# A transformer block pair on one core: x by features, projections ahead of its norm

## The chip, the core and the metric

The kernel runs on one core of a Trainium2 chip. The metric is device time in microseconds (us). The engines are called PE (TensorE), DVE (VectorE), ACT (ScalarE), POOL (GpSimd) and SP (SyncE, which here only issues transfers).

## The reference

Two transformer blocks are applied to x, 512 tokens of 1024 features, all fp32. What the change touches is the first stage of the first block, and a filter that the second block needs:

```python
h = rms_norm(x, g_mix_pre)                 # x * rsqrt(mean(x*x) + eps) * gain, per token
proj = h @ w_in                            # 1024 x 5376
q, k, v, p_in, gm_u, gm_v, gate_in = split(proj)
o_sb = stick_breaking_attention(q, k, v)
o_pool = multiscale_pool(p_in, ...)        # trailing sums over tokens
o_gm = gelu(gm_u) * (W_s @ norm(gelu(gm_v)) + b)
...
h = sin(freq * (z @ w1 + b1)); h = sin(freq * (h @ w2 + b2)); h = sin(freq * (h @ w3 + b3))
h = (h @ w4) * exp(-t * deltas)            # 512 taps x 2048: filters of the second block
```

The norm's factor is one number per token, the gain one per feature. So `(x * gain) @ w * factor` equals `rms_norm(x) @ w`.

## The kernel before

**Products in two halves.** Each fp32 operand of a large product is split into a rounded high part and a low part (fp32r); a product is three matmuls of 512 columns, high by high, high by low, low by high (`mm3`, line 460). Weights come as units of 128x1024 (0.5 MB): SP loads a unit into one of four `RAW` buffers (line 2552), ACT copies it rounded to `WH` (line 1108, semaphore `w_hi`), DVE subtracts to `WL` (line 1687, `lo`). There are four slots of each, so unit u waits until PE has begun unit u-3 (`w_used`). Each engine's own program says by a call `weights(u)` where among its other work it handles unit u, and it works strictly in that order.

**The start.** SP issues four transfers for x by tokens (0.5 MB each), the constants, `pp` (per-feature numbers), four weight units, and the filter's inputs. ACT squares and sums x (line 1122); DVE scales x by its norm's factor (line 1702); PE turns it with 32 transposes (`turn_x`, line 521, 16 of them within the first projection); ACT and DVE read the turned tiles from PSUM, times the gain, into `HTh` and `HTl` (lines 1130, 1708), eight tiles of 128 features by 512 tokens.

**The first stage** is a loop over k = 0..19 in each of the four programs; each k has a `first(k)` and a `second(k)`. On PE:

- k = 0 to 3: one block of `w_in` for p_in (k 0, 1) or gm_u (k 2, 3), 24 matmuls (`feature_group`, line 534, units 0 to 3). ACT brings the result out of PSUM, with gelu for gm_u (lines 1139, 1141).
- k = 4: first gm_v (`token_step`, 96 matmuls of 256 columns, units 4 and 5), then block 0 of q and k. k = 4 to 11 are the eight blocks j = k - 4 of q and k, one unit each (6 to 13). ACT copies a block out (line 1151), DVE subtracts (line 1721).
- k = 12 to 19: v (units 14 to 17), and at 16 to 19 a `mix` product of the pooled and the gated branch.

`second(k)` on PE is one layer of the filter network at k = 0, 1, 2 (`filter_layer`, line 568: a small fp32 matmul, then seven DVE instructions, lines 1733 to 1742, then a Sin on ACT, line 1163), and one of eight tap steps at k = 3 to 10 (`taps`, line 579). A tap step t is a pair of fp32 matmuls into banks 6 and 7. DVE multiplies both by the decay (line 1753, `tap_mul`), into two buffers; POOL writes their sum and difference (line 2359, `tap_ed`); SP stores them (line 2597). Step t may use the banks on PE once DVE has read step t-1, and DVE may write the buffers once POOL is done with step t-1. Steps 2i and 2i+1 use one decay, an Exp of 128x2048 on ACT into a single buffer (line 1170), taken after DVE's last use of the one before. After the last tap step POOL computes the trailing sums (line 2369), which the mix at k = 16 needs.

The attention's scores begin at k = 18, and all that follows is in the order that PE's program gives.

Of the kernel before, what the change touches and what calls it, by code (L numbers as in the profile page):

```python
# [7 lines left out]
F32R = mybir.dt.float32r  # L8
# [156 lines left out]
class Waits:  # L165
# [5 lines left out]
    def wait_ge(self, name, n):  # L171
        s, before = self.find(name)
        if n > 0 and self.past.get(s.name, 0) < before + n:
# [14 lines left out]
          "lp": tuple((n, 2) for n in ("nc", "n3", "n4")),  # L188
# [5 lines left out]
CHAINS = {"p_turn": (("p_n1", 8), ("p_n2", 8), ("p_nc", 4), ("p_n3", 8), ("p_n5", 4), ("p_n4", 8)),  # L194
# [8 lines left out]
          "p_subn": (("p_sub", 1), ("p_sn", 4)),  # L203
# [4 lines left out]
          "v_gate": (("eg_raw", 6), ("eg_mul", 4), ("ef_v", 8), ("g_mul", 18)),  # L208
# [15 lines left out]
          "g_wide": (("o2_xp", 6), ("dn_xp", 14)),  # L224
          "p_qk2": (("p_q2", 4), ("p_kx", 4)),
# [45 lines left out]
def program(nc, a):  # L271
    ctx = ExitStack()
    with ctx:
# [21 lines left out]
        SPL = [at("spl", k, [P, 1280], F32R) for k in (10, 168)]  # L295
        WT = [at("wt", 3 * i, [P, 6, P]) for i in range(2)]
# [9 lines left out]
        DELT, DEC = at("delt", 128, [P, CHUNK]), at("dec", 144, [P, CHUNK])  # L306
# [129 lines left out]
        def tensor_program(engine):  # L436
# [82 lines left out]
            e.wait_ge("d_c", 32)  # L519

            def turn_x(k):
                b = bank(("n1", k), "n1_lo", k + 1, tuple(range(8)))
                for i in range(4):
                    e.wait_ge("n1_xn", i + 1)
                    m = tp(PS[:, b, i * P:(i + 1) * P], Y[:, i, k * P:(k + 1) * P])
                m.then_inc(sem("p_n1"), 1)

            for k in range(4):
                turn_x(k)


            RING6, RING2 = tuple(range(6)), (6, 7)

            def feature_group(key, s, n, c, ready, done):
                b = bank(key, s, n, RING6)
                for k in KT:
                    if key == ("proj", 0) and k < 4:
                        turn_x(k + 4)
                    e.wait_ge(ready, k + 1)
                    m = mm3(PS[:, b, :], weights("w_in", k * P, c), HT(k), k == 0, k == 7)  # L540
                m.then_inc(sem(done), 1)

            def token_step(key, k, c, w, done):
                wk = weights("w_in", k * P, c)
                for i in range(4):
                    h, l = HT(k)
                    m = mm3(PS[:, BANK[key, i], :w], (h[:, i * P:(i + 1) * P], l[:, i * P:(i + 1) * P]), wk, k == 0, k == 7)
                    if k == 7:
                        m.then_inc(sem(done), 1)

            def first(k):
                if k < 4:
                    feature_group(("proj", k), "proj_ev", k + 1, 1536 + k * P, "n1_lo", "p_proj")
                elif k < 12:
                    if k == 4:
                        for i in range(4):
                            bank(("gmv", i), "gmv_ev", i + 1, RING6)
                        for kk in KT:
                            token_step("gmv", kk, 2048, 256, "p_gmv")
                    j = k - 4  # L560
                    feature_group(("qk", j), "qk_lo", j + 1, j * P, "n1_lo", "p_qk")
                else:
# [3 lines left out]
                    token_step("v", k - 12, 1024, S, "p_v")  # L566
# [12 lines left out]
            def taps(i, o):  # L579

                n = 4 * i + 2 * o
# [512 lines left out]
        def scalar_program(engine):  # L1094
# [29 lines left out]
            e.wait_ge("d_c", 32)
            weights(0)
            for k in KT:
                if k % 4 == 0:
                    weights(k // 4)
                e.wait_ge("p_n1", k + 1)
                act(HTh[:, k, :], PS[:, BANK["n1", k], :], ACT.Copy, scale=pp("g_mix_pre", k)).then_inc(sem("n1_hi"), 1)  # L1130
            act(SILU, pp("c_2", 0, 16), ACT.Silu).then_inc(sem("silu"), 1)
# [1666 lines left out]
```

## Time and profile before

| | us |
|---|---|
| median of 3 runs | 1540.36 (1539.1 to 1541.3) |
| the profiled execution | 1541.3 |
| its span | 1539.5 |
| TensorE busy in it | 1482.3 (96%) |
| TensorE's mean granted clock | 0.988 of full |

The page gives each engine's busy time, a view of the span in 40 slices, the transfer queues, the chain of work that ended last, and the costliest groups of instructions. Beside it the trace was read as a timeline of each engine, in groups by line, and in stages (busy time of each engine in a stretch). Times are us from the span's start. A matmul's duration in the timeline reaches over the start of the next one; the distance from start to start is what it costs.

### The profile page before, as it was taken

To read this page: it belongs to the slowest core of one execution; us is meant where nothing else is said; L and a number is where in the kernel's file an instruction comes from. 1 tells how busy PE (TensorE), PEld (TensorE's weight loads), DVE (VectorE), ACT (ScalarE), POOL (GpSimd) and SP (SyncE) were. 2 spreads that over 40 slices of the span, in tenths; PEclk is the share of its full clock that TensorE was granted. 3 is DMA by queue.
4 is the path that set the end of the run, shared out by engine and by line. 5 is a ranking of instruction groups with operands and counts; after the bars stand their busy time and mean duration, and the time that the engine had idled before them with its cause. 6 is when DMAs were issued, how large, how long until landed. Compare 5 with 4: busy or idle time off the path is not lost.

```text
span 1539.5 us, 18009 instructions
## 1 busy us (share of the span) xinstructions
PE 1482.3 (96%) x7022; PEld 1205.6 (78%) x7022; DVE 862.8 (56%) x1397; ACT 620.6 (40%) x986; POOL 311.0 (20%) x297
## 2 busy tenths in 40 slices
PE   6999999999989999999998999999898999999998
PEld 5776768888778878888876878877687888888886
DVE  5455667554567565574457437777656545345434
ACT  5645763232444222334335326653445333123332
POOL 0263211101032100121004312225620111111101
PEclk9999999999999999999999999999999999999999
DMA  7352105655245354545326221233432232322321
GB/s 256 112 164 69 42 28 187 211 163 170 77 161 182 129 170 144 173 150 178 119 87 218 86 69 42 61 102 125 161 126 96 96 96 96 107 86 95 106 86 55
DMA packets 53327, 187.93 MB, mean 122 GB/s; under 512 B 5943, under 2 KB 6616, under 8 KB 53114
## 3 DMA queue, kind: packets, MB, share of 16 engines
q1 hardware_dynamic: 47450, 165.80, 32.8%
q0 software_dynamic: 4736, 16.78, 3.3%
q10 hardware_dynamic: 1056, 4.19, 0.8%
q8 instruction: 56, 0.92, 0.2%
q14 instruction: 29, 0.24, 0.1%
HBM read 174.16 MB, written 12.58 MB: 121 GB/s over the span
## 4 chain that ended last, share of the span: by engine, by line
PE 88%; DVE 6%; ACT 3%; issue 2%; DMA 0%; POOL 0%; SPq 0%; ACTq 0%; DVEq 0%; POOLq 0%
PE PS L458 87%; PE PS L469 2%; DVE wl L1687 1%; ACT wh L1108 1%; ACT TMP L1202 1%; DVE TMP L2182 0%; ACT TMP L1200 0%; DMA X<-in_x 0%; DVE TMP L1740 0%; DVE accm L1667 0%; DVE Y L1898 0%; DVE TMP L2145 0%; DVE HTl L2009 0%; ACT TMP L1213 0%; ACT TMP L1396 0%
## 5 line engine op out<-in xcount | busy, mean ns | idle before, releaser
L1687 DVE TENSOR_TENSOR wl<-raw,wh 128x1024 fp32r<-128x1024 f32 x211 | 273.2, 1299 | 283.6 <-ACT wh L1108 283.3
L458 PE MATMUL PS<-HTh,wh 128*128 128x512 f32 x1056 | 419.7, 397 | 6.5 <-ACT TMP L1396 3.9
L458 PE MATMUL PS<-HTl,wh 128*128 128x512 f32 x1056 | 413.7, 392 | 0.0
L458 PE MATMUL PS<-HTh,wl 128*128 128x512 f32 x1056 | 413.7, 392 | 0.0
L1108 ACT ACTIVATE wh<-raw 128x1024 fp32r<-128x1024 f32 x228 | 239.1, 1052 | 281.5 <-PE PS L458 246.3
L458 PEld LDWEIGHTS PS<-HTh,wh 128*128 128x128 f32 x1056 | 199.8, 189 | 54.1 <-issue 10.5
L458 PEld LDWEIGHTS PS<-HTh,wl 128*128 128x128 f32 x1056 | 199.5, 189 | 43.2
L458 PEld LDWEIGHTS PS<-HTl,wh 128*128 128x128 f32 x1056 | 199.7, 189 | 39.1 <-issue 0.5
L458 PE MATMUL PS<-wh,FFh 128*128 128x512 f32 x432 | 169.9, 393 | 0.0
L458 PE MATMUL PS<-wl,FFh 128*128 128x512 f32 x432 | 168.7, 390 | 0.0
L458 PE MATMUL PS<-wh,FFl 128*128 128x512 f32 x432 | 168.7, 390 | 0.0
L1667 DVE SCALAR_TENSOR_TENSOR accm<-raw,small,accm 128x256 f32<-128x256 f32 x224 | 108.1, 517 | 3.4
L2282 DVE SCALAR_TENSOR_TENSOR TMP<-PS,pp,TMP 128x255 f32<-128x255 f32 (+1 forms) x132 | 52.1, 395 | 78.6 <-ACT TMP L1619 74.7
L458 PEld LDWEIGHTS PS<-wh,FFl 128*128 128x128 f32 x432 | 81.5, 189 | 17.2
L458 PEld LDWEIGHTS PS<-wl,FFh 128*128 128x128 f32 x432 | 81.6, 189 | 16.7
L458 PEld LDWEIGHTS PS<-wh,FFh 128*128 128x128 f32 x432 | 81.5, 189 | 16.6
L2436 POOL TENSOR_TENSOR FFl<-TMP,FFh 128x512 fp32r<-128x512 f32 x32 | 41.6, 1300 | 240.3 <-ACT FFh L1330 240.3
L2517 POOL TENSOR_TENSOR FFl<-TMP,FFh 128x512 fp32r<-128x512 f32 x22 | 28.5, 1295 | 210.1 <-ACT FFh L1626 210.1
L2322 POOL TENSOR_TENSOR wl<-raw,wh 128x1024 fp32r<-128x1024 f32 x17 | 42.5, 2505 | 113.7 <-ACT wh L1108 113.7
L1330 ACT ACTIVATE FFh<-TMP 128x512 fp32r<-128x512 f32 x32 | 20.2, 633 | 66.6 <-DVE TMP L1958 66.6
L1326 ACT ACTIVATE TMP<-PS 128x512 f32<-128x512 f32 x32 | 19.1, 595 | 57.3 <-PE PS L458 57.3
L2525 POOL TENSOR_TENSOR X<-X,TMP 128x512 f32<-128x512 f32 x14 | 19.7, 1440 | 90.1 <-DVE TMP L2297 90.1
(322 smaller groups left out, 2132.9 us busy)
## 6 DMA issues: line engine op xcount, KB each, us to landing
raw<-in_ws SPq DMA_DIRECT2D x268, 512.0 KB, 3.8
taps<-TMP SPq DMA_DIRECT2D x16, 256.0 KB, 2.5
tab<-in_spec POOLq DMA_DIRECT2D x8, 512.0 KB, 5.6
raw<-taps SPq DMA_DIRECT2D x8, 512.0 KB, 3.8
kd<-TMP POOLq DMA_DIRECT2D x16, 256.0 KB, 5.4
wh<-in_wd POOLq DMA_DIRECT2D x8, 512.0 KB, 4.0
wl<-in_wd POOLq DMA_DIRECT2D x8, 512.0 KB, 4.6
kf<-kd SPq DMA_DIRECT2D x8, 512.0 KB, 3.7
```

The costliest lines, as they stand in the source:

```text
L458: return nc.tensor.matmul(out, l, r, start=start, stop=stop, skip_group_check=True)
L469: return nc.tensor.transpose(out, in_, IDENT)
L1108: act(WH[u % SLOTS][:, :n], RAW[i % RAWS][:, :n], ACT.Copy).then_inc(sem("w_hi"), 1)
L1326: act(T(q % 2), PS[:, BANK["ff", hf, m], :], ACT.Relu).then_inc(sem("ff_relu"), 1)
L1330: act(FFh[:, m, :], T(2 + q % 2), ACT.Copy).then_inc(sem("ff_hi"), 1)
L1667: stt(acc, r[:, k % 4, :], c, acc, ALU.mult, ALU.add).then_inc(sem("mod_acc"), 1)
L1687: tt(WL[k][:, :n], RAW[RAW_AT["unit", u, 0] % RAWS][:, :n], f32(WH[k][:, :n]), ALU.subtract).then_inc(sem("lo_dve"), 1)
L2282: stt(z[:, do], ps[:, di], pp("ffn_conv_w_2", 22 * w + m), z[:, do], ALU.mult, ALU.add).then_inc(sem("uc_v"), 1)
L2322: tt(WL[k][:, :n], RAW[RAW_AT["unit", u, 0] % RAWS][:, :n], f32(WH[k][:, :n]), ALU.subtract).then_inc(sem("lo_pool"), 1)
L2436: tt(FFl[:, q % 16, :], T(2 + q % 2), f32(FFh[:, q % 16, :]), ALU.subtract).then_inc(sem("ff_lo"), 1)
L2517: tt(FFl[:, m - first_m, :], T(m % 4), f32(FFh[:, m - first_m, :]), ALU.subtract).then_inc(sem("ug_lo"), 1)
L2525: tt(x, x, T(4 + q % 4), ALU.add).then_inc(sem("dn_xp"), 1)
```

## The change

- x is also laid out by features in memory (`xt`), and SP loads it first: pp, XT tiles 0 and 1, weight unit 0, tiles 2 to 7, unit 1, then x by tokens with units 2 and 3 in it, then the constants and the filter's inputs. `turn_x` and its 32 transposes are gone.
- ACT and DVE split x times gain into `HUh` and `HUl`, tile by tile. The four projections of k = 0 to 3 and gm_v are computed from these, ahead of the norm's factor. The factor is spread over all partitions by one fp32 matmul in the middle of k = 2 (`factor_spread`) and copied to `RS`. DVE takes k = 0 to 3 out of PSUM times `RS` (`projected`); gm_v gets the factor as ACT's scale.
- For q, k, v and the gates, `HTh` and `HTl` are made from XT: DVE multiplies by gain and `RS`, ACT rounds, POOL subtracts (`normed`).
- The filter's layers move: layer 0 after k = 1, layer 1 in the middle of k = 3, layer 2 in the middle of gm_v. On DVE and ACT all three stand, with `projected`, `normed` and the weights' halves, in a written order ahead of the loop.
- The tap steps are two to a block at k = 5 to 8, one in the middle and one at the end (`TAPS_AT`). The decays have two buffers; the first is taken ahead of the loop, the others at the end of k = 4, 5, 6.
- The gelu of gm_u and the Silu of c move on ACT behind gm_v's.

The diff, cut to its core:

```diff
 # PE
-            for k in range(4):
-                turn_x(k)
+            def feature_group(key, s, n, c, ready, done, xs, middle=None):
                 b = bank(key, s, n, RING6)
                 for k in KT:
-                    if key == ("proj", 0) and k < 4:
-                        turn_x(k + 4)
+                    if k == 4 and middle:
+                        middle()
...
                 if k < 4:
+                    feature_group(("proj", k), "proj_x", k + 1, 1536 + k * P, "raw_lo", "p_proj", HU,
+                                  {2: factor_spread, 3: lambda: filter_layer(1)}.get(k))
...
                         for kk in KT:
-                            token_step("gmv", kk, 2048, 256, "p_gmv")
+                            if kk == 4:
+                                filter_layer(2)
+                            token_step("gmv", kk, 2048, 256, "p_gmv", HU)
                     j = k - 4
+                    t = TAPS_AT(k)
+                    feature_group(("qk", j), "qk_lo", j + 1, j * P, "n1_lp", "p_qk", HT, (lambda: taps(t[0])) if t else None)
+            def factor_spread():
+                b = bank("rs", "rs_ev", 1, RING2)
+                e.wait_ge("d_c", 16)
+                e.wait_ge("rdg", 4)
+                mm(PS[:, b, :], ONES, RDG[:, :], True, True).then_inc(sem("p_rs"), 1)
             def second(k):
-                if k < 3:
-                    filter_layer(k)
-                elif k < 11:
-                    taps(*divmod(k - 3, 2))
+                if k == 1:
+                    filter_layer(0)
+                for t in TAPS_AT(k)[1:]:
+                    taps(t)
+        def TAPS_AT(k):
+            return range(2 * k - 10, 2 * k - 8) if 5 <= k < 9 else ()
 # ACT
+            for k in KT:
+                e.wait_ge(f"d_xt{k // 2}", 16)
+                act(HUh[:, k, :], XT[:, k, :], ACT.Copy, scale=pp("g_mix_pre", k)).then_inc(sem("raw_hi"), 1)
+                if k == 1:
+                    weights(0)
+            weights(1)
             for i in range(4):
...
+                act(SQX[:, :], X[:, i, :], ACT.Square, accum_out=N1[:, i:i + 1]).then_inc(sem("n1_sq"), 1)
+                if i == 1:
+                    weights(2)
             root(N1[:, 8:12], N1[:, 0:4], D, "n1_sq", 4).then_inc(sem("n1_rt"), 1)
+            weights(3)
+            e.wait_ge("p_rs", 1)
+            act(RS[:, :], PS[:, BANK["rs"], :], ACT.Copy).then_inc(sem("rs_ev"), 1)
+            def decay(i):
+                if i > 1:
+                    e.wait_ge("tap_mul", 4 * (i - 1))
+                act(DEC[i % 2][:, :], DELT[:, :], ACT.Exp, scale=pp("negt", i)).then_inc(sem("dec"), 1)
+            filter_layer(0)
+            weights(4)
+            normed(range(4))
+            weights(5)
+            filter_layer(1)
+            weights(6)
+            normed(range(4, 8))
+            weights(8)
+            e.wait_ge("d_w4", 48)
+            e.wait_ge("n1_lp", 8)
+            decay(0)
+            filter_layer(2)
             def first(k):
                 if k < 4:
+                    pass
                 elif k < 12:
                     if k == 4:
                         weights(unit("w_in", 7 * P, 2048) + SLOTS - 1)
+                        e.wait_ge("n1_r", 1)
                         for i in range(4):
                             e.wait_ge("p_gmv", i + 1)
+                            act(GV[:, i, :], PS[:, BANK["gmv", i], :256], ACT.Gelu_apprx_tanh,
+                                scale=N1[:, 12 + i:13 + i]).then_inc(sem("gmv_ev"), 1)
+                        e.wait_ge("proj_x", 4)
+                        for i in range(2):
+                            act(GU[:, i, :], GU[:, i, :], ACT.Gelu_apprx_tanh).then_inc(sem("proj_ev"), 1)
+                        act(SILU, pp("c_2", 0, 16), ACT.Silu).then_inc(sem("silu"), 1)
                     j = k - 4
                     weights(unit("w_in", 0, j * P) + SLOTS - 1)
                     e.wait_ge("p_qk", j + 1)
...
             def second(k):
+                if 4 <= k < 7:
+                    decay(k - 3)
 # DVE
+            for k in KT:
+                e.wait_ge("raw_hi", k + 1)
+                stt(HUl[:, k, :], XT[:, k, :], pp("g_mix_pre", k), f32(HUh[:, k, :]), ALU.mult,
+                    ALU.subtract).then_inc(sem("raw_lo"), 1)
+                if k == 1:
+                    weights(0)
+            weights(2)
...
+                ts(RDG[:, i * P:(i + 1) * P], IDENT, N1[:, 12 + i:13 + i], None, ALU.mult).then_inc(sem("rdg"), 1)
+            weights(3)
+            def projected(ks):
+                for k in ks:
+                    e.wait_ge("p_proj", k + 1)
+                    e.wait_ge("rs_ev", 1)
+                    to = PT[:, k, :] if k < 2 else GU[:, k - 2, :]
+                    tt(to, PS[:, BANK["proj", k], :], RS[:, :], ALU.mult).then_inc(sem("proj_x"), 1)
+            def normed(ks):
+                for k in ks:
+                    e.wait_ge("raw_lo", k + 1)
+                    stt(XT[:, k, :], XT[:, k, :], pp("g_mix_pre", k), RS[:, :], ALU.mult, ALU.mult).then_inc(sem("n1_xn"), 1)
...
                     weights(unit("w_in", 0, j * P) + SLOTS - 1)
+                    for t in TAPS_AT(k)[:1]:
+                        taps(t)
                     e.wait_ge("qk_hi", j + 1)
...
             def second(k):
+                for t in TAPS_AT(k)[1:]:
+                    taps(t)
...
+            filter_layer(0)
+            projected((0, 1, 2))
+            weights(4)
+            normed(range(4))
+            weights(5)
+            filter_layer(1)
+            weights(6)
+            normed(range(4, 8))
+            weights(7)
+            projected((3,))
+            filter_layer(2)
             for k in range(20):
                 first(k)
 # POOL
+            for k in KT:
+                e.wait_ge("n1_hi", k + 1)
+                tt(HTl[:, k, :], XT[:, k, :], f32(HTh[:, k, :]), ALU.subtract).then_inc(sem("n1_lp"), 1)
             e.wait_ge("dec", 1)
...
             e.wait_ge("tap_ed", 16)
-            e.wait_ge("proj_ev", 2)
+            e.wait_ge("proj_x", 2)
 # SP
+            engine.dma_start(PPT[:, :], a["pp"]).then_inc(sem("d_p"), 16)
+            for i in range(4):
+                engine.dma_start(XT[:, 2 * i:2 * i + 2, :], a["xt"][:, 2 * i:2 * i + 2, :]).then_inc(sem(f"d_xt{i}"), 16)
+                if i in (0, 3):
+                    load()
             for i in range(4):
                 engine.dma_start(X[:, i, :], a["x"][i * P:(i + 1) * P, :]).then_inc(sem(f"d_x{i}"), 16)
+                if i % 2:
+                    load()
```

## Rows read from the trace of the kernel before

**Rows 1.** The page's busy times and its chain that ended last, whole run.

```profile
PE 1482.3 (96%) x7022; PEld 1205.6 (78%) x7022; DVE 862.8 (56%) x1397; ACT 620.6 (40%) x986; POOL 311.0 (20%) x297
...
PE 88%; DVE 6%; ACT 3%; issue 2%; DMA 0%; POOL 0%; SPq 0%; ACTq 0%; DVEq 0%; POOLq 0%
```

**Rows 2.** Busy times of each engine by stage, core 0, with granted clock and DMA.

```profile
core 0: us, PE busy (x) PEld busy (x) DVE busy (x) ACT busy (x) POOL busy (x), PEclk, DMA share, GB/s
...
58.70:106.05 47.35, 47.35 (x199) 33.26 (x198) 22.23 (x28) 18.82 (x20) 21.79 (x13) 1.00 0.52 161
...
141.00:144.00 3.00, 1.62 (x13) 1.05 (x13) 0.69 (x1) 2.23 (x5) 1.28 (x1) 1.00 0.00 0
144.00:150.00 6.00, 5.40 (x21) 3.93 (x21) 3.42 (x7) 4.33 (x13) 1.13 (x4) 0.52 0.29 87
```

**Rows 3.** Timeline from 0 to 20: start, us, engine, line, operation, [idle before].

```profile
4.45 1.06 ACT L1122 ACTIVATE Y<-X 128x1024 f32<-128x1024 f32 x1 [2.35 <-DMA X<-in_x]
...
8.70 1.06 ACT L1122 ACTIVATE Y<-X 128x1024 f32<-128x1024 f32 x1 [0.15 <-DMA X<-in_x]
...
11.69 1.06 ACT L1108 ACTIVATE wh<-raw 128x1024 fp32r<-128x1024 f32 x1 [1.60 <-DMA raw<-in_ws]
...
13.13 3.89 PE L469 MATMUL PS<-cst,Y 128*128 128x128 f32 x17 [0.19 <-DVE Y L1702]
...
16.67 0.78 PE L458 MATMUL PS<-HTh,wh 128*128 128x512 f32 x1
...
19.18 0.60 PE L469 MATMUL PS<-cst,Y 128*128 128x128 f32 x4
```

**Rows 4.** Groups by line from 10 to 130: busy us, mean ns.

```profile
L2359 POOL TENSOR_TENSOR TMP<-TMP 128x512 f32<-128x512 f32 x16 | 28.9, 1824 | 29.1 <-DVE TMP L1753 29.1
...
L1108 ACT ACTIVATE wh<-raw 128x1024 fp32r<-128x1024 f32 x20 | 20.9, 1051 | 10.0 <-PE PS L458 8.4 <-DMA raw<-in_ws 1.6
...
L1170 ACT ACTIVATE dec<-delt,pp 128x2048 f32<-128x2048 f32 x4 | 8.0, 2002 | 0.0
...
L1151 ACT ACTIVATE QKh<-PS 128x512 fp32r<-128x512 f32 x8 | 4.8, 598 | 29.1 <-PE PS L458 29.1
```

**Rows 5.** ScalarE's timeline from 45 to 58.

```profile
45.13 0.63 ACT L1163 ACTIVATE TMP<-TMP 128x512 f32<-128x512 f32 x1 [2.36 <-DVE TMP L1742]
...
48.63 1.28 ACT L1170 ACT_TABLE_LOAD   x1
49.93 2.00 ACT L1170 ACTIVATE dec<-delt,pp 128x2048 f32<-128x2048 f32 x1
...
57.80 1.46 ACT L1147 ACTIVATE bc<-PS 128x256 f32<-128x256 f32 x4 [2.14 <-PE PS L458]
```

**Rows 6.** VectorE's timeline, 26 to 94.

```profile
26.42 0.81 DVE L1733 TENSOR_SCALAR TMP<-PS,pp 128x512 f32<-128x512 f32 x1
...
30.36 0.43 DVE L1742 TENSOR_SCALAR TMP<-TMP 128x512 f32<-128x512 f32 x1
...
75.53 1.29 DVE L1753 TENSOR_TENSOR TMP<-PS,dec 128x512 f32<-128x512 f32 x2 [3.12 <-ACT dec L1170]
...
80.45 1.29 DVE L1753 TENSOR_TENSOR TMP<-PS,dec 128x512 f32<-128x512 f32 x2 [1.30 <-POOL TMP L2359]
...
93.95 2.33 DVE L1687 TENSOR_TENSOR wl<-raw,wh 128x1024 fp32r<-128x1024 f32 x1
```

**Rows 7.** GpSimd's timeline from 93.

```profile
93.91 3.52 POOL L2359 TENSOR_TENSOR TMP<-TMP 128x512 f32<-128x512 f32 x2 [1.95 <-DVE TMP L1753]
```

**Rows 8.** TensorE's timeline at the second and the last pair of taps.

```profile
64.24 1.13 PE L458 MATMUL PS<-w,TMP 64*128 64x512 f32 x4
...
104.68 1.13 PE L458 MATMUL PS<-w,TMP 64*128 64x512 f32 x4
105.74 0.50 PE L458 MATMUL PS<-HTh,wh 128*128 128x512 f32 x1
```

**Rows 9.** Line 1687: duration ns min/median/max.

```profile
L1687 DVE TENSOR_TENSOR wl<-raw,wh x211: 1202/1226/2332, 13.0 to 1512.0; 128x1024 fp32r<-128x1024 f32 x106
```

More of the change, by code:

```diff
@@ L305, in program @@
         MTh, MTl = QKh, QKl
[L306 removed]
+        DELT, DEC = at("delt", 128, [P, CHUNK]), [at("dec", k, [P, CHUNK]) for k in (144, 136)]
         SKIP = at("skip", 152, [1, D])
@@ L516, in HT, with HU, token_step @@
                 return tile(HTh, HTl, k)
[L519 to L526, printed above, removed]
-            for k in range(4):
-                turn_x(k)
             RING6, RING2 = tuple(range(6)), (6, 7)
-            def feature_group(key, s, n, c, ready, done):
+            def HU(k):
+                return tile(HUh, HUl, k)
+            def feature_group(key, s, n, c, ready, done, xs, middle=None):
                 b = bank(key, s, n, RING6)
                 for k in KT:
-                    if key == ("proj", 0) and k < 4:
-                        turn_x(k + 4)
+                    if k == 4 and middle:
+                        middle()
                     e.wait_ge(ready, k + 1)
-                    m = mm3(PS[:, b, :], weights("w_in", k * P, c), HT(k), k == 0, k == 7)
+                    m = mm3(PS[:, b, :], weights("w_in", k * P, c), xs(k), k == 0, k == 7)
                 m.then_inc(sem(done), 1)
-            def token_step(key, k, c, w, done):
+            def token_step(key, k, c, w, done, xs):
                 wk = weights("w_in", k * P, c)
+                h, l = xs(k)
                 for i in range(4):
-                    h, l = HT(k)
                     m = mm3(PS[:, BANK[key, i], :w], (h[:, i * P:(i + 1) * P], l[:, i * P:(i + 1) * P]), wk, k == 0, k == 7)
@@ L577, in filter_layer, with taps @@
                 mm(PS[:, b, :], TMP[0:n, 1, P * l:P * (l + 1)], src, True, True).then_inc(sem("p_filt"), 1)
-            def taps(i, o):
-                n = 4 * i + 2 * o
+            def taps(t):
+                i, o = divmod(t, 2)
+                n = 2 * t
                 for d in range(2):
@@ L1123, in scalar_program @@
             root(N1[:, 8:12], N1[:, 0:4], D, "n1_sq", 4).then_inc(sem("n1_rt"), 1)
[L1124 to L1131, printed above, removed]
+            weights(3)
@@ L1700, in vector_program, with normed @@
             e.wait_ge("n1_r", 1)
+            e.wait_ge("d_c", 16)
             for i in range(4):
-                ts(Y[:, i, :], X[:, i, :], N1[:, 12 + i:13 + i], None, ALU.mult).then_inc(sem("n1_xn"), 1)
-            e.wait_ge("d_c", 32)
-            for k in KT:
-                if k % 4 == 0:
-                    weights(k // 4)
-                e.wait_ge("n1_hi", k + 1)
-                stt(HTl[:, k, :], PS[:, BANK["n1", k], :], pp("g_mix_pre", k), f32(HTh[:, k, :]), ALU.mult,
-                    ALU.subtract).then_inc(sem("n1_lo"), 1)
+                ts(RDG[:, i * P:(i + 1) * P], IDENT, N1[:, 12 + i:13 + i], None, ALU.mult).then_inc(sem("rdg"), 1)
[6 more added lines that the diff above has]
+                    tt(to, PS[:, BANK["proj", k], :], RS[:, :], ALU.mult).then_inc(sem("proj_x"), 1)
+            def normed(ks):
+                for k in ks:
+                    e.wait_ge("raw_lo", k + 1)
+                    stt(XT[:, k, :], XT[:, k, :], pp("g_mix_pre", k), RS[:, :], ALU.mult, ALU.mult).then_inc(sem("n1_xn"), 1)
             def first(k):
                 if k < 4:
-                    weights(unit("w_in", 0, 1536 + k * P) + SLOTS - 1)
+                    pass
                 elif k < 12:
@@ L2591, in sync_program @@
                     weights(unit("w_in", (k - 12) * P, 1024) + SLOTS - 1)
-                if 3 <= k < 11:
-                    t = k - 3
+                for t in TAPS_AT(k):
                     for x in range(2):
```

74 lines of the change are left out of this document (29 added, 45 removed), and 7 rows, old and new, of the table SHARED.

## The prediction

> **What bounds the kernel now.** The page first: TensorE is busy 96% of the span and holds 88% of the chain that ended last, VectorE 6% and ScalarE 3% [rows 1]. So a microsecond is won only where TensorE begins earlier or waits less, and lost where the change makes it wait. The stages show where that can be. From 58.7 to 106.05, the q and k blocks with the tap steps, TensorE is busy all of 47.35 us, VectorE 22.2, ScalarE 18.8, POOL 21.8 [rows 2]. The gap is at the start: real products begin at 16.67, behind the transposes at 13.13 [rows 3]. Around 142 TensorE has a short wait, 1.62 busy of 3 us, and then runs six microseconds at a granted clock of 0.52, that is mostly at 1.2 GHz [rows 2]. Later stages follow TensorE's order, so I carry the shift at the end of the q and k blocks to the end.
>
> **1. The start.** x lands from 4.45 to 8.70, three more half megabytes in 4.25 us, 1.42 each; weight unit 0 at 11.69, 3.0 behind the last for 0.9 MB [rows 3]. In the new order, at 1.4 each and 0.4 for pp ahead: XT's first pair about 5.1, unit 0 6.5, the last pair 10.7, unit 1 12.1, x by tokens 13.5 to 19.1, units 2 and 3 16.3 and 20.5, constants and filter inputs 21.2 to 21.7. All sit in one queue of SP, so x's last tile comes 10 us later than before; nothing but the factor waits for it. ScalarE takes 1.05 for unit 0 [rows 4], VectorE 1.22 [rows 9]: the first product is at 8.9, 7.8 earlier.
>
> Projection 0 then needs the eight `HUl`, at 0.7 us each up to about 12.8. 24 matmuls cost 5.45 (six blocks with a pair of taps each from 64.24 to 104.68 are 6.74 apiece, a pair 1.3 with its ramp [rows 8]). The transposes at 13.13 cost 0.23 apiece, those at 19.18 0.15 [rows 3], so TensorE was slow for its first five microseconds of work. I give projection 0 till 16.5, projection 1 till 22.0. Filter layer 0 (1.1, as a pair of taps [rows 8]) finds its inputs there. Projection 2 with the factor's matmul (1.1 likewise) ends at 29.7: x's last tile 19.1, its square, root, reciprocal and four small products with the identity, some 3 us, are in time. Projection 3 with layer 1 ends at 36.3. Before, gm_v began at 47.1 with layer 2 and tap step 0 behind it, 2.3 us of work that is now still to come. The lead is 47.1 - 2.3 - 36.3 = 8.5.
>
> **2. The relay of VectorE and ScalarE.** The two now hand each other everything in a written order. From projection 2's end on: VectorE `projected` 0.7, unit 4 1.2, four `normed` 2.9, unit 5 1.2, layer 1's seven instructions 4.3 (26.42 to 30.79 [rows 6], my count for each layer), then ScalarE's Sin 0.63 [rows 5] and unit 6 1.05 [rows 4], VectorE unit 6 1.2, four `normed` 2.9, ScalarE the last `HTh` 0.63 and unit 7 1.05, VectorE unit 7 1.2, `projected` 0.7, layer 2 4.3. Sum 24.0: layer 2 leaves VectorE at 53.7 if POOL is out of the way. It isn't: the eight `HTl` are GpSimd instructions that read SBUF, and a half of the weights that takes 1.2 took 2.33 at 93.95, beginning just behind POOL's at 93.91 [rows 6, 7, 9]. One such instruction is 1.3 (3.52 for two with VectorE's between). Eight are 10.4; those that fall where VectorE waits for ScalarE are free. I take 5.5 and keep 0 and 8 as bounds: 59.2.
>
> The Trainium skill, SBUF — State Buffer, section Who interferes with whom, says that a VectorE instruction with two SBUF inputs contends with a GpSimd instruction that reads SBUF and that the later one is blocked whole. The 2.33 agrees. By this rule `normed` and three of a layer's instructions block and are blocked as the weights are, as I count; if it held for weights alone, 0 to 2 of the 5.5 would be left.
>
> TensorE meanwhile: layer 2 in the middle of gm_v (at 42.1) wants Sin 1, which comes at about 44 (29.7 + 0.7 + 1.2 + 2.9 + 1.2 + 4.3 + 0.6 + 3 for POOL), a wait of 2. gm_v (11.4, 47.3 to 58.7) ends at 51, block 0 at 56.4, half of block 1 at 59.1. There tap step 0 wants Sin 2. On ScalarE decay 0 stands ahead of it, waiting for the last `HTl` (56), then 2.0 and a table load on either side of Sin, 1.28 each [rows 5]: Sin 2 is there at 61.2. Step 0 ends at 62.4, block 1 at 65.1.
>
> **3. The long wait.** Step 1 stands at the end of block 1. Its banks are free when VectorE has read step 0. But VectorE's step 0 stands behind unit 10's low half, and ScalarE's unit 10 behind all of k = 4: table load 1.28, gm_v's four gelus 1.46, gm_u's two 1.2, table load 1.28, Silu 0.2, unit 9 1.05, q's block 0.6, table load 1.28, decay 1 2.0, unit 10 1.05 [rows 4, 5]. That is 11.4, some 10.8 with their overlaps: 61.2 to 72.0. VectorE adds unit 10 1.22, a product 0.65, the skip row 0.7 and a product 0.65 [rows 6, 9]: 75.2. TensorE waits from 65.1 to 75.2, ten microseconds, and the lead is gone. Before, these same instructions of ScalarE lay beside blocks without a tap step that hung on them. Queued behind VectorE's wait are q's first low half and unit 11, whose users come later.
>
> **4. Two steps to a block.** A step is a pair of products on VectorE, 1.29, and two instructions of POOL, 2.6 alone and 3.5 with a weights' half between, together 4.1 to 4.9 (75.53 to 80.45 [rows 6]); POOL's line has a mean of 1.82 [rows 4]. TensorE offers one each 2.72 + 1.3 = 4.0, where before it offered one each 6.74. So the steps now set the pace: six from 75.2 at 4.8 (decays 2 and 3 wait for their buffers in the same order), the last at 104.0, its pair done at 105.1. Before it was done at 105.74, but with one block left and not three [rows 8]. Two blocks are 10.9: the q and k blocks end 105.1 - 105.74 + 10.9 = 10.3 later. Bounds of this term: -4.2 at 4.1 a step, +1 at 5.0.
>
> What follows is unchanged in order. POOL's sums, 13 us behind the last step, are in time for the mix at k = 16, now some 28 us away. Costed at nothing: the second decay buffer, squares into another tile, gelus of gm_u from SBUF; each lies in ScalarE's time counted above or where VectorE and ScalarE are half idle [rows 2]. The clock after a ten-microsecond wait: by 144 to 150 six microseconds near half speed, up to 3 us [rows 2], most of it inside the steps' own pace; range 0 to 3, I take 0. If the dip around 144 goes, that gives back up to 3.
>
> **The sum** is 1541.3 (the profiled execution; span 1539.5) + 10.3 = 1551.6. That execution is 0.94 above the median of 1540.36, so 1550.6.
>
> The Trainium skill, ScalarE: Activation LUTs, section What ACT_TABLE_LOAD costs, states 1283 ns and a drain of some 1380 for every switch. By it the four loads in the relay would add 5.5 to mine. The trace speaks against: load at 48.63, the Exp begins at 49.93 [rows 5].
>
> **The rivals.**
>
> A, the lead survives: faster. The wait of step 1 is under two microseconds because VectorE reads step 0 early. What is left is 8.5, less 2 for layer 2, less 1 to 3 for the steps' pace: 1535 to 1538. For it: all of ScalarE's work to 106 is under half of the time. Against: order, not load, makes the wait; it would turn only if Sin 2 came ahead of about 51, and the relay without any POOL contention puts layer 2 at 53.7. Chance 0.07; 0.02 more for no change by some mixture.
>
> B, POOL costs the relay little: Sin 2 at about 56, the rest equal, 5 us less: 1543 to 1547. For it: before, VectorE's long weights' half appears only a few times (median 1.23 [rows 9]). Chance 0.18.
>
> C, switches of tables dearer, or POOL's instructions at 1.8 as in its tap line [rows 4] so that Sin 1 and Sin 2 both slip: 3 to 6 more, 1554 to 1557. Chance 0.13. A part of it is the page's drain.
>
> D, the forecast, 1547 to 1554: 0.60.
>
> **How the numbers follow.** Within 0.2% is within 3.1 us, about what a measurement of this kernel tells from nothing. Faster 0.07, same 0.03 (with B's edge), slower 0.90. The range takes in B, D and most of C: 1544 to 1556.
>
> **What would show it.** First product near 9, gm_v's start near 36; transposes gone; a wait of TensorE near 65 of 8 to 11 us ended by VectorE's line of the tap products; ScalarE in the order above ahead of it; then short waits at each step; two more blocks of q and k behind the last step; everything from the scores on shifted by one constant. It is wrong if TensorE has no wait above 3 us before 110, or if Sin 2 comes before 52.

## The result and the profile after

The changed kernel takes 1552.33 us (median of 4 runs, 1550.28 to 1552.75) against 1539.73 (4 runs, 1539.01 to 1541.3) on the same chip: ratio 1.0077, interval 1.0065 to 1.0089. It is 12.6 us slower. 1550.6 was forecast, the range was 1544 to 1556. The profiled execution took 1552.3, its span is 1550.5, 11.0 over before's: before's profiled execution, 1541.3, was the slowest of its four.

The page's busy times and chain, which answer to [rows 1]. TensorE's work is the same, the span is longer:

```profile
PE 1482.6 (96%) x6992; PEld 1204.5 (78%) x6992; DVE 869.0 (56%) x1409; ACT 623.4 (40%) x992; POOL 317.9 (21%) x305
...
PE 85%; DVE 6%; ACT 4%; issue 2%; POOL 2%; DMA 0%; SPq 0%; DVEq 0%; ACTq 0%; POOLq 0%
```

What TensorE waited for most from 5 to 170 (in total, times, longest):

```profile
PE PS L468 <- DVE wl L1726: 11.6, 1, 11.6
PE PS L468 <- DVE TMP L1812: 10.2, 4, 7.9
PE PS L468 <- ACT TMP L1154: 2.1, 1, 2.1
...
```

The 11.6 is the start itself. L1812 is VectorE's products with the decay, L1154 the Sin.

TensorE's timeline: the first product, layer 2's matmul, tap steps 0, 1, 3 and 5, to be read beside [rows 3, 8]:

```profile
11.58 0.76 PE L468 MATMUL PS<-HUh,wh 128*128 128x512 f32 x1 [11.58 <-DVE wl L1726]
...
47.23 2.04 PE L468 MATMUL PS<-TMP 64*128 64x512 f32 x2 [2.10 <-ACT TMP L1154]
...
65.42 1.13 PE L468 MATMUL PS<-w,TMP 64*128 64x512 f32 x4
...
77.38 2.08 PE L468 MATMUL PS<-w,TMP 64*128 64x512 f32 x4 [7.87 <-DVE TMP L1812]
...
87.50 1.13 PE L468 MATMUL PS<-w,TMP 64*128 64x512 f32 x4 [0.20 <-DVE TMP L1812]
...
96.93 1.13 PE L468 MATMUL PS<-w,TMP 64*128 64x512 f32 x4 [1.32 <-DVE TMP L1812]
```

The last step, not shown, is at 105.88 with a wait of 0.85.

The first product is 5.1 earlier than before. Step 0 waits for nothing. Step 1, one half block later, waits 7.87 for VectorE's reading of step 0. ScalarE's timeline ahead of that wait, all of it one list:

```profile
61.00 1.28 ACT L1154 ACT_TABLE_LOAD   x1
62.30 0.63 ACT L1154 ACTIVATE TMP<-TMP 128x512 f32<-128x512 f32 x1
62.94 1.28 ACT L1189 ACT_TABLE_LOAD   x1
64.24 1.57 ACT L1189 ACTIVATE bc<-PS,smallring 128x256 f32<-128x256 f32 x4
65.68 1.16 ACT L1193 ACTIVATE gu<-gu 128x512 f32<-128x512 f32 x2
66.86 1.28 ACT L1194 ACT_TABLE_LOAD   x1
68.15 0.22 ACT L1194 ACTIVATE small<-pp 128x16 f32<-128x16 f32 x1
68.28 1.04 ACT L1121 ACTIVATE wh<-raw 128x1024 fp32r<-128x1024 f32 x1
69.23 0.58 ACT L1198 ACTIVATE QKh<-PS 128x512 fp32r<-128x512 f32 x1
69.82 1.28 ACT L1165 ACT_TABLE_LOAD   x1
71.11 2.00 ACT L1165 ACTIVATE dec<-delt,pp 128x2048 f32<-128x2048 f32 x1
73.02 1.04 ACT L1121 ACTIVATE wh<-raw 128x1024 fp32r<-128x1024 f32 x1
```

VectorE's timeline of the same time. Its step 0 (L1812) stands behind unit 10's half, which waits for the last line above:

```profile
69.35 1.23 DVE L1726 TENSOR_TENSOR wl<-raw,wh 128x1024 fp32r<-128x1024 f32 x1 [6.89 <-ACT wh L1121]
...
74.09 1.22 DVE L1726 TENSOR_TENSOR wl<-raw,wh 128x1024 fp32r<-128x1024 f32 x1 [2.92 <-ACT wh L1121]
75.23 0.68 DVE L1812 TENSOR_TENSOR TMP<-PS,dec 128x512 f32<-128x512 f32 x1
75.95 0.68 DVE L1816 TENSOR_TENSOR TMP<-TMP,skip 1x512 f32<-1x512 f32 x1
76.56 0.67 DVE L1812 TENSOR_TENSOR TMP<-PS,dec 128x512 f32<-128x512 f32 x1
```

Stages (columns as in [rows 2]). From 48 to 56 TensorE is busy but slow, behind its wait of 2.10; from 76 to 80 it is idle and then slow. The stage 70 to 110 holds 9.7 us of idle where before had none:

```profile
48.00:52.00 4.00, 4.00 (x15) 2.81 (x14) 3.94 (x5) 1.92 (x4) 1.31 (x1) 0.50 0.34 122
52.00:56.00 4.00, 4.00 (x28) 4.00 (x28) 2.35 (x2) 2.53 (x3) 4.00 (x4) 0.75 0.02 9
...
70.00:110.00 40.00, 30.26 (x113) 18.67 (x114) 20.22 (x29) 14.35 (x13) 18.74 (x15) 0.91 0.45 157
...
76.00:80.00 4.00, 2.62 (x6) 1.05 (x7) 1.93 (x4) 0.00 (x0) 2.49 (x2) 0.50 0.52 184
```

The shift is read best from the last q/k block leaving PSUM. After the change, and then the same moment before it:

```profile
123.61 0.60 ACT L1198 ACTIVATE QKh<-PS 128x512 fp32r<-128x512 f32 x1 [3.89 <-PE PS L468]
```

```profile
111.53 0.60 ACT L1151 ACTIVATE QKh<-PS 128x512 fp32r<-128x512 f32 x1 [4.13 <-PE PS L458]
```

So 12.1 later, and the span 11.0. "Last block" below means this moment.

### The profile page after: what moved, and what is told of

Read it like the earlier page. It is cut to its first block, busy times and chain, and to the rows that moved or that the text cites. A ratio compares the mean times of both kernels' runs of the same rounds, so it can differ in the third digit from the quotient of the medians.

```text
span 1550.5 us, 17988 instructions
## 1 busy us (share of the span) xinstructions
PE 1482.6 (96%) x6992; PEld 1204.5 (78%) x6992; DVE 869.0 (56%) x1409; ACT 623.4 (40%) x992; POOL 317.9 (21%) x305
## 4 chain that ended last, share of the span: by engine, by line
PE 85%; DVE 6%; ACT 4%; issue 2%; POOL 2%; DMA 0%; SPq 0%; DVEq 0%; ACTq 0%; POOLq 0%
PE PS L468 84%; PE PS L479 1%; POOL TMP L2430 1%; ACT wh L1121 1%; DVE wl L1726 1%; ACT TMP L1241 1%; DVE TMP L2250 0%; DMA raw<-in_ws 0%; ACT TMP L1239 0%; POOL HTl L2419 0%; DVE accm L1706 0%; DVE Y L1966 0%; DVE xt L1765 0%; ACT dec L1165 0%; DVE TMP L2213 0%
## 5 line engine op out<-in xcount | busy, mean ns | idle before, releaser
L468 PE MATMUL PS<-HTh,wh 128*128 128x512 f32 x1024 | 407.2, 398 | 6.5 <-ACT TMP L1435 3.9
L468 PE MATMUL PS<-HTl,wh 128*128 128x512 f32 x1024 | 401.6, 392 | 0.0
L468 PE MATMUL PS<-HTh,wl 128*128 128x512 f32 x1024 | 401.4, 392 | 0.0
L468 PEld LDWEIGHTS PS<-HTh,wh 128*128 128x128 f32 x1024 | 194.1, 190 | 52.7 <-issue 9.8
L468 PEld LDWEIGHTS PS<-HTh,wl 128*128 128x128 f32 x1024 | 193.8, 189 | 41.6
L468 PEld LDWEIGHTS PS<-HTl,wh 128*128 128x128 f32 x1024 | 194.1, 190 | 38.0 <-issue 0.5
L2588 POOL TENSOR_TENSOR FFl<-TMP,FFh 128x512 fp32r<-128x512 f32 x22 | 28.5, 1294 | 211.2 <-ACT FFh L1665 211.2
```

The lines of the kernel that those rows point to most:

```text
L468: return nc.tensor.matmul(out, l, r, start=start, stop=stop, skip_group_check=True)
L2588: tt(FFl[:, m - first_m, :], T(m % 4), f32(FFh[:, m - first_m, :]), ALU.subtract).then_inc(sem("ug_lo"), 1)
```

## The experiments

Each was timed beside the kernel before (medians of 1540.2 to 1541.1), and the ratios are to that. The changed kernel was not timed again beside them: it lay 12.6 over the kernel before, so 7.2 over it, as in the first experiment, is 5.4 won, while the medians themselves differ by 4.4. Below, what an edit gives is the difference of the medians. Each ratio's interval reaches 1 to 2 us to either side, so gains under some 3 us are not clear of noise by the medians alone. Diffs are cut, and against the changed kernel unless said otherwise.

Traces differ between executions too. With the same start the first product came between 10.3 and 11.7, and TensorE's low clock behind a wait is in some executions and not in others.

### Read step 0 ahead of unit 9's half

```diff
 # DVE, first(k)
+                    if k == 4:
+                        taps(0)
                     weights(unit("w_in", 0, j * P) + SLOTS - 1)
                     for t in TAPS_AT(k)[:1]:
-                        taps(t)
+                        if t:
+                            taps(t)
```

> VectorE reads tap step 0 right behind filter layer 2 and unit 8, ahead of unit 9's low half; nothing else moves. Theory 'order' (the wait at 69.4 is VectorE standing behind ScalarE's list for k = 4): step 0 is read by about 68, TensorE passes step 1 without a wait, and the wait moves to step 2, because step 1 is read only behind unit 10's half (75.3): step 1's read ends about 77 where it ended at 81.9. So 4 to 5 us less than the changed kernel: about 1548. Theory 'load' (VectorE, ScalarE and POOL have too much to do for two steps in a block, whatever the order): less than 1 us, 1551 to 1553.

Measured 1547.89 (1544.61 to 1548.21, 5 runs), ratio 1.0040 (1.0028 to 1.0052). TensorE, steps 1 and 2:

```profile
66.96 1.13 PE L468 MATMUL PS<-w,TMP 64*128 64x512 f32 x4
77.09 2.08 PE L468 MATMUL PS<-w,TMP 64*128 64x512 f32 x4 [6.04 <-DVE TMP L1815]
```

The wait goes from step 1 and stands at step 2, 1.8 shorter, since ScalarE's list is the same. Last block 118.59, 5.0 earlier. (The profiled execution, 1544.6, was the fastest of its five; it has no low clock around 150, where the changed kernel lost 3.1.) VectorE's step 0 in another place of its order gives back 4.4 us, as expected: order made the wait, not load.

### Layer 2's matmul later

```diff
-                            if kk == 4:
-                                filter_layer(2)
+ # and as the middle of q/k block 0: filter_layer(2)
```

> TensorE's matmul of filter layer 2 moves from the middle of gm_v to the middle of q and k block 0. VectorE begins layer 2 only at 57.0 by its own list, so nothing of the relay moves. Theory 'relay' (VectorE and ScalarE set the end of the stage): TensorE loses its wait of 2.1 us at 45 and most of the slow clock from 46 to 54, comes to tap steps 0 and 1 that much earlier and waits that much longer: 1551.5 to 1552.5, no change. Theory 'TensorE' (its waits add up): 4 to 5 us less, about 1548.

Measured 1552.78 (1551.58 to 1555.16, 5 runs), ratio 1.0080 (1.0067 to 1.0093): nothing gained, as its first theory had it. TensorE no longer waits at 47, but 1.8 for Sin 2 at step 0 and 8.55 at step 1, at 77.60 where it was 77.38. TensorE's lateness ahead of Sin 2 costs nothing; the relay behind it sets the end.

### ScalarE's list shortened

```diff
 # ACT: decay(1) right behind decay(0), ahead of Sin 2;
 # gelu of gm_u and Silu moved:
+                elif k == 9:
+                    e.wait_ge("proj_x", 4)
+                    for i in range(2):
+                        act(GU[:, i, :], GU[:, i, :], ACT.Gelu_apprx_tanh).then_inc(sem("proj_ev"), 1)
+                    act(SILU, pp("c_2", 0, 16), ACT.Silu).then_inc(sem("silu"), 1)
```

> ScalarE's list between Sin 2 and unit 10 is made shorter: the gelu of gm_u and the Silu (1.2 + 1.3 + 0.2 us) go behind k = 9, and decay 1 (2.0, with its table load 1.3) goes directly behind decay 0, ahead of Sin 2. Theory 'order': Sin 2 comes 2.0 later (64.9, still ahead of TensorE's step 0 at 65.4), unit 10's high half 3.9 earlier (70.1 for 74.1), the long wait 4 us instead of 8: about 1548. Theory 'load': the same work is still on ScalarE ahead of the end of the stage, so no change.

Measured 1549.75 (1547.89 to 1553.99, 6 runs), ratio 1.0064 (1.0051 to 1.0076); last block 119.46. Expected was 1548; the 2.6 won is not clear of noise. Step 1 comes at 73.23 with a wait of 4.54, but step 0 now waits 2.66 for Sin 2. Part of the list only changed sides: the decay moved ahead of Sin 2 puts it 1.4 later (64.35 where it was 62.93). The rest is that TensorE was not slowed after layer 2 in this execution and was at step 0 at 61.94, 3.5 earlier; with the decay in its old place (next experiment) step 0 waited 0.76.

### Steps spread over k = 5 to 10

```diff
-            return range(2 * k - 10, 2 * k - 8) if 5 <= k < 9 else ()
+            return {5: (0,), 6: (1, 2), 7: (3,), 8: (4, 5), 9: (6,), 10: (7,)}.get(k, ())
```

Decays 2 and 3 are taken one k later.

> The eight tap steps stand at k = 5 (0), 6 (1, 2), 7 (3), 8 (4, 5), 9 (6), 10 (7) instead of two each at k = 5 to 8, decays 2 and 3 one k later. Step 1 is wanted 2.7 us later, so the long wait is 5.3 instead of 8; the short waits from 84 to 108 (2.4 us in all) go, since a step is now offered each 5.4 us and costs VectorE and POOL 4.1 to 4.9. Theory 'pace of the steps is part of the loss': 4 to 5 us less, about 1547.5. If only the first wait counts: 2.7 less, about 1549.6.

Measured 1548.89 (1547.4 to 1550.5, 5 runs), ratio 1.0054 (1.0042 to 1.0066). The median lies between the two that were expected (1547.5 and 1549.6). The long wait stays: 7.42 at step 1, 76.81, and not 5.3, since TensorE, not slowed after layer 2 in this execution, was at step 0 at 61.84 and so at step 1 early. Behind it no step waits, and a block and a half stand behind the last step at 109.36: last block 118.92.

### The kernel before, with the steps two to a block

Edit, on the kernel before: only `TAPS_AT` as in the change, with its two decay buffers; start, layers and norm as before.

> The kernel before with one part of the change alone: tap steps two to a block at k = 5 to 8, one in the middle and one at the end, and two buffers of decays, taken at k = 3 to 6. Start, transposes and filter layers as before. Its filter is ready by 46, so no list of ScalarE stands ahead of step 0. Theory 'pace' (a step costs VectorE and POOL 4.1 to 4.9 and is offered each 4.0, with one step of slack): waits of 1 to 3 us in all, 1541.5 to 1543.5. Theory 'two to a block is the main loss': 6 us or more, from 1546.5 on. If it costs nothing: 1540.5.

Measured 1545.73 (1545.12 to 1549.17, 5 runs) against 1541.07, ratio 1.0036 (1.0023 to 1.0048): 4.7 us, about twice the upper end of what was expected. The trace is of the slowest of the five, 1549.2, whose first product came 1.0 later than before's; its last block is at 117.92, 6.4 later. TensorE's waits for VectorE's products from 5 to 170:

```profile
PE PS L462 <- DVE TMP L1762: 5.6, 5, 1.5
```

And VectorE between steps 1 and 2:

```profile
74.22 0.69 DVE L1762 TENSOR_TENSOR TMP<-PS,dec 128x512 f32<-128x512 f32 x1 [2.10 <-POOL TMP L2368]
74.94 0.68 DVE L1766 TENSOR_TENSOR TMP<-TMP,skip 1x512 f32<-1x512 f32 x1
75.55 0.67 DVE L1762 TENSOR_TENSOR TMP<-PS,dec 128x512 f32<-128x512 f32 x1
79.24 1.23 DVE L1694 TENSOR_TENSOR wl<-raw,wh 128x1024 fp32r<-128x1024 f32 x1 [3.02 <-ACT wh L1116]
80.39 1.28 DVE L1762 TENSOR_TENSOR TMP<-PS,dec 128x512 f32<-128x512 f32 x2
```

The pair of a block waits for POOL, then the next step waits behind a weights' half that ScalarE hands over late. The pairing is a loss without the new start too.

### Steps 0 and 1 read early, without and with the spread

Both have layer 2 late, gelu of gm_u and Silu at k = 9, and VectorE reads steps 0 and 1 ahead of unit 9's half; the second has the spread as well.

> The changed kernel with three things moved: VectorE reads tap steps 0 and 1 ahead of unit 9's low half, filter layer 2's matmul stands in block 0, and the gelu of gm_u and the Silu come behind k = 9. Two steps to a block stay. Theory 'order': both early reads free the banks at 66 and 71, so TensorE's only long wait is for Sin 2 (about 3 us at 60), and the pace of the steps does the rest: last q and k block done about 112 (111.5 before, 123.6 in the changed kernel), 1541. Theory 'load': 1546 or more.

> As the one above, and the steps spread at k = 5 (0), 6 (1, 2), 7 (3), 8 (4, 5), 9 (6), 10 (7). By 'order' and 'pace' together no wait is left behind Sin 2: step 0 from 63, then half a block, six blocks and seven pairs, 44.5 us: the last block ends about 108.7, 2.8 earlier than before: 1537 to 1538.5, faster than both kernels. If the lead of the start is lost in some other place, 1540 or more.

Measured 1548.23 (1545.18 to 1548.71, 5 runs), ratio 1.0041 (1.0028 to 1.0054), and 1543.17 (1541.13 to 1546.38, 11 runs), ratio 1.0013 (1.0004 to 1.0022). Both missed, by 7 and by 5 to 6. The first lies where its rival 'load' had put it (1546 or more), but its trace shows an order again: reading step 1 early piles three weights' halves up behind it. VectorE in the first of the two:

```profile
71.65 1.20 DVE L1726 TENSOR_TENSOR wl<-raw,wh 128x1024 fp32r<-128x1024 f32 x1
...
73.39 1.70 DVE L1726 TENSOR_TENSOR wl<-raw,wh 128x1024 fp32r<-128x1024 f32 x1
...
75.61 1.72 DVE L1726 TENSOR_TENSOR wl<-raw,wh 128x1024 fp32r<-128x1024 f32 x1
77.25 1.27 DVE L1816 TENSOR_TENSOR TMP<-PS,dec 128x512 f32<-128x512 f32 x2
```

Step 3 then waits 2.00, step 4 2.49, step 5 1.37. With the spread a wait of 2.60 is left at step 3, beside 1.83 for Sin 2. That load does not force them is shown by the last kernel below, which does the same work without them.

### All four edits

Step 0 alone read early, layer 2 late, decay 1 and the gelus moved, the steps spread.

> The first four edits in one: VectorE reads step 0 early (step 1 in its old place), layer 2's matmul in block 0, decay 1 ahead of Sin 2 and gelu of gm_u and Silu late, steps spread. If the pieces measured alone (4.5, 0, 3, 3.5 us) added up: 1541. By 'order' Sin 2 comes 2.0 later than without decay 1 in front (64.9), and the last block ends about 111: 1539.5 to 1541. Against the one above it tells what decay 1's place costs.

Measured 1542.20 (1540.76 to 1543.91, 11 runs), ratio 1.0007 (0.9999 to 1.0016). Expected was 1539.5 to 1541, so it missed by 1.2; 10.1 of the 12.6 have come back in the medians. In the trace the last block is at 111.91, where before has 111.53 and the changed kernel 123.61: nearly the 12 us have come back, by order alone. One wait above 0.7 is left, step 0's for Sin 2, which two decays now precede. TensorE's timeline, and the stage behind the wait (columns as in [rows 2]), four slow microseconds:

```profile
64.44 1.13 PE L468 MATMUL PS<-w,TMP 64*128 64x512 f32 x4 [3.72 <-ACT TMP L1153]
```

```profile
66.00:70.00 4.00, 4.00 (x13) 3.10 (x12) 3.50 (x5) 3.45 (x6) 2.34 (x2) 0.57 0.01 2
```

### Two tries at the last wait

Against the kernel with all four edits: the steps one k later, steps 2 and 5 two, decays 2 and 3 at k = 7 and 9. The second kernel has besides `normed(range(4, 8))` ahead of filter layer 1 and unit 6.

```diff
-            return {5: (0,), 6: (1, 2), 7: (3,), 8: (4, 5), 9: (6,), 10: (7,)}.get(k, ())
+            return {6: (0,), 7: (1,), 8: (2, 3), 9: (4,), 10: (5, 6), 11: (7,)}.get(k, ())
```

> The kernel of all four edits (1542.2), with every tap step but one put one block of q and k later: steps at k=6 (middle), 7 (middle), 8 (both), 9 (middle), 10 (both), 11 (middle), decays 2 and 3 at k=7 and 9. There TensorE came to step 0 at 60.7 and waited 3.7 for Sin 2. Now it comes at about 66, behind Sin 2 (64.2). Theory, that this wait was all that was left of the loss: no wait above 1 us before 110, last q and k block out of PSUM near 108.2 (111.9 - 3.7), median 1538.5. Rival, that order only moves the wait: it turns up at step 2 or 3 or, since the last step is now behind and POOL's sums 13 us after it, at the blocks of v; median 1541 or more.

> The same, and the second four of normed ahead of filter layer 1 and unit 6 on VectorE and ScalarE. Theory: the last HTl comes some 4 us earlier, so the 0.7 that block 0 waits for it goes; layer 1 comes 4 us later, at about 50, and nothing waits for it since layer 2's matmul stands at about 58. Median 1537.8, 0.7 below the kernel beside it. Rival: layer 2 and Sin 2 come later than 66 because unit 6 and 7 pile up behind POOL's eight in a row, and step 0 waits again: no gain, 1539 to 1541.

Measured 1548.03 (1547.34 to 1548.82, 5 runs), ratio 1.0051 (1.0037 to 1.0065), and 1551.36 (1548.35 to 1552.23, 5 runs), ratio 1.0067 (1.0055 to 1.0080). The first fell to its rival (order only moves the wait: 1541 or more), by more than that named. The second missed theory and rival (1539 to 1541) alike: Sin 2 did come later than 66, but step 0 does not wait for it; the wait is elsewhere. TensorE in the first:

```profile
66.28 0.50 PE L468 MATMUL PS<-HTh,wh 128*128 128x512 f32 x1 [2.60 <-ACT bc L1189]
...
107.99 2.08 PE L468 MATMUL PS<-w,TMP 64*128 64x512 f32 x4 [3.34 <-DVE TMP L1817]
```

At 63.7 block 2 wants a PSUM bank that gm_v's gelus (L1189) give back, and these stand behind the two decays and Sin 2. At k = 9 decay 3, the gelus and Silu in a row delay a weights' half, behind which VectorE's step 5 stands, and step 6 waits for that. In the second, block 0 waits 5.20 for unit 6's half, which now stands behind the eight `normed` and layer 1, and step 6's 3.34 is there as well.

### gm_v's gelus ahead of the decays

Against the kernel with all four edits:

```diff
 # ACT, behind weights(8)
+            e.wait_ge("n1_r", 1)
+            for i in range(4):
+                e.wait_ge("p_gmv", i + 1)
+                act(GV[:, i, :], PS[:, BANK["gmv", i], :256], ACT.Gelu_apprx_tanh, ...)
             e.wait_ge("d_w4", 48)
...
-            return {5: (0,), 6: (1, 2), 7: (3,), 8: (4, 5), 9: (6,), 10: (7,)}.get(k, ())
+            return {6: (0,), 7: (1, 2), 8: (3,), 9: (4, 5), 10: (6, 7)}.get(k, ())
```

VectorE's step 0 stands ahead of k = 5's half, its step 1 at the end of k = 6; gelu of gm_u and Silu at k = 11, decays 2 and 3 at k = 7 and 8.

> The kernel of all four edits (1542.2) with the order of ScalarE mended where the kernel with later steps showed its next wait: block 2 of q and k wants a bank that the gelus of gm_v leave, and these stood behind decays 0 and 1 and Sin 2. Now gm_v's gelus stand ahead of decay 0, in 2 to 3 us in which ScalarE waited for the last HTl; step 0 is in the middle of k=6, the others at 7 (both), 8, 9 (both), 10 (both); VectorE reads steps 0 and 1 ahead of a weights' half; gelu of gm_u and Silu at k=11. Theory, that what is left is ScalarE's list ahead of Sin 2 and gm_v's banks, and nothing of the hardware: Sin 2 at 65, before TensorE's step 0 at 66; no wait above 1 us before 110; last block at 108; median 1538. Rival, that the two engines' written order always has a next item: a wait of 2 to 4 us turns up again between 66 and 100 and the median is 1541 or more.

Measured 1538.8 (1537.38 to 1541.94, 11 runs) against 1540.18 (1538.76 to 1541.39, 15 runs), ratio 0.9994 (0.9985 to 1.0003); 1538 was expected. TensorE's waits for VectorE's products and for `HTl` from 5 to 170, and then ScalarE's timeline at the last q/k block:

```profile
PE PS L468 <- DVE TMP L1816: 0.9, 2, 0.5
PE PS L468 <- POOL HTl L2425: 0.7, 1, 0.7
```

```profile
106.75 0.60 ACT L1194 ACTIVATE QKh<-PS 128x512 fp32r<-128x512 f32 x1 [4.12 <-PE PS L468]
```

The last block is 4.8 earlier than before; the first product, at 10.27 in this execution, was 6.4 earlier. No microsecond up to the last block ran at the low clock. Of the 4.8 the span kept 3.2 (1536.3): its waits for ScalarE (L1253) from 105 to 200 are 3.2, against 2.4 before (L1213); the rest I have not traced. In the medians 1.4 is left, which the interval does not tell from nothing. So no version here is shown to beat the kernel before, but the loss of the change is shown to be order alone: the same work (6992 matmuls on TensorE, 1409 instructions on VectorE), 13.5 us less.

## Why the prediction was right

**The sum.** The forecast put the change 10.3 us over the kernel before, at 1550.6; it came 12.6 over in the medians (12.0 over the 1540.36 that it started from) and 11.0 in the profiled spans. Up to the last block the shift was 12.1, and 1.1 of it went again behind it, where the forecast had a constant.

**The start** was mis-sized. The first product came at 11.58, not 8.9: XT's first pair had landed at 5.77 and unit 0 at 9.12, where 5.1 and 6.5 were taken. Transfers issued first did not land at the pace of [rows 3]. ScalarE at the start:

```profile
5.77 1.33 ACT L1137 ACTIVATE HUh<-xt,pp 128x512 fp32r<-128x512 f32 x2 [3.66 <-DMA xt<-in_xt]
9.12 1.06 ACT L1121 ACTIVATE wh<-raw 128x1024 fp32r<-128x1024 f32 x1 [2.02 <-DMA raw<-in_ws]
```

The lead was 5.1, not 7.8, and gm_v began at about 39 (36.3 forecast). It changed nothing in the sum, since the relay covers TensorE until step 1; it would have made rival A 2.7 slower.

**The relay** ran in the order written down. Projection 2 was read by VectorE at 32.69 (29.7), the start's lateness handed on; layer 2 left VectorE at 61.3 (59.2), and Sin 2 was there at 62.93 (61.2). What held Sin 2 was the path over POOL, as forecast: its last `HTl` was done at 57.60 (56), then table load, decay, table load and Sin. POOL's price, taken as 5.5 within 0 to 8, was about 3.2 on VectorE's halves and `normed`: two halves at 1.84 for 1.22, and two groups of four `normed` at 3.8 for 2.8 (four of 0.7, as the forecast had them). VectorE and POOL in that stretch:

```profile
34.59 3.79 DVE L1765 SCALAR_TENSOR_TENSOR xt<-xt,pp,rs 128x512 f32<-128x512 f32 x4
40.02 1.84 DVE L1726 TENSOR_TENSOR wl<-raw,wh 128x1024 fp32r<-128x1024 f32 x1 [1.65 <-ACT wh L1121]
```

```profile
36.08 6.95 POOL L2419 TENSOR_TENSOR HTl<-xt,HTh 128x512 fp32r<-128x512 f32 x4 [35.55 <-ACT HTh L1160]
```

Of the Trainium skill's rule (SBUF — State Buffer, Who interferes with whom) this supports the part that was in doubt: `normed` pays as the halves do, and POOL pays too, four instructions in 6.95 where 1.3 apiece makes 5.2. A half loses 0.6 here, half of one POOL instruction; whether it was blocked for the rest of one that had begun, or slowed, the trace does not tell.

**Layer 2's wait** was 2.10 (2 forecast). **The long wait** stands at step 1, for VectorE's read of step 0, behind the list named: from Sin 2 to the end of unit 10's `WH` it took 11.1 us (62.93 to 74.06; 10.8 forecast). It was 7.9 and not 10, just under the 8 to 11 that were named as its sign, because TensorE came to step 0 only at 65.42: the start's 2.7, and 3.3 lost at the low clock from 47 to 54. That is the term I had at 0; added up microsecond by microsecond (busy time by one less the granted clock) it is 5.3 up to the last block, and 0.0 before. 3.3 of it were hidden by the relay. 2.0 fell between steps 1 and 2 (77.38 and 83.22), where VectorE's read of step 1, done at 81.9, hid a part. Step 1 itself came at 77.38 (75.2).

**The pace** was 4.75 a step ((105.88 - 77.38) / 6; 4.8 forecast), the last step at 105.88 (104.0), with two more blocks behind it than before. That this came so near is in part luck. The forecast had VectorE and POOL hold every step; measured, TensorE's own 4.02 (87.50 to 91.52) set steps 4 and 6, and six times 4.02 is 24.1 of the 28.5. The rest is waits of 0.20, 1.32 and 0.85 at steps 3, 5 and 7, and the 2.0 of slow clock behind step 1, which the forecast had at 0 beside the pace. And the waits at 3 and 5 came from the order again: VectorE's read of steps 2 and 4 stood behind a weights' half that waited for ScalarE, which had a decay ahead of it. VectorE ahead of its read of step 4:

```profile
94.36 1.23 DVE L1726 TENSOR_TENSOR wl<-raw,wh 128x1024 fp32r<-128x1024 f32 x1 [3.02 <-ACT wh L1121]
```

Of the reads that TensorE waited for, only that of step 6 waited for POOL, 2.53.

Last block +12.1 (+10.3): the 1.8 are the relay's and the list's lateness. The dip around 144 stayed, 12 us later, with the same 3.1 us lost.

**The table loads.** Each load took 1.28 and the next instruction began 1.29 to 1.30 behind its start, as in [rows 5]. The drain that the Trainium skill adds (ScalarE: Activation LUTs, What ACT_TABLE_LOAD costs) is not seen at any of the loads from 61 to 71. From the last `HTl` to the long wait's release there are five loads, not the four that the forecast's sentence on that page counted; its own sum has all five.

**Rival A** (the lead survives) needed Sin 2 ahead of 51. Measured, that condition was wrong: with Sin 2 begun at 63.51 the last kernel has no wait above 0.7 before its last block, since steps can also move back and ScalarE's order can change.

## What to carry to other kernels

When several engines run by lists written out by hand, a head start is worth what the next hand-over lets through: write down for each wait everything that stands ahead of the releasing instruction, on its engine and on the one that this waits for. An engine that is half idle can still hold another up for 8 us by where its next instruction stands; put first what frees a bank or a buffer, and move long lists of things that nobody waits for behind it. Change such an order with a trace of each step: here the four edits gave 0 to 4.4 us one by one and 10 together, and two that were to remove the last wait lost 6 to 9 of these again.

## What was not expected of the hardware

The granted clock fell to 0.50 for three to seven microseconds behind some waits of TensorE, and not behind others of the same length. Behind layer 2's wait of 2.1 it fell in the changed kernel (3.3 us lost) and in the kernel with step 0 read early (1.7), and not at all in the kernels with ScalarE's list shortened and with the steps spread. In the first kernel with steps 0 and 1 read early it fell behind the 1.84 for Sin 2 (1.7 lost) and not behind 2.00 and 2.49. In the kernel before it fell behind waits of 0.30 and 1.08 between 141 and 144 (3.1 lost); in the kernel before with pairs five waits of 0.6 to 1.5 ahead of the last block lost nothing. Longer waits: 3.72 with all edits (1.7), 7.87 at 77 (2.0). So the length of one wait does not tell whether the clock falls; where it fell behind one it cost 1.6 to 3.3 beside the wait. What decides it no run here shows.

At the start TensorE was slow without that column showing it: from 11.58 to 16.41 products began some 0.43 apart and from 16.66 on 0.23, while the granted clock reads 1.00 from 11 to 19. The forecast had five slow microseconds from the transposes, and that held.

POOL's two instructions of a tap step took 2.5 with no weights' half on VectorE beside them, 3.4 to 3.5 with one [rows 7], and 4.4 where several followed each other (the first kernel with steps 0 and 1 read early, at 71.80).
